# A fused four-layer kernel with the step order of all engines written out anew

## What is computed

```python
def first_block(x, ...):
    for layer in range(2):
        h = rmsnorm(x, norm_mix_g[layer])
        if layer % 2 == 0:
            mix = retention_nsa_mixer(h, ...)      # retention (4 heads) and NSA attention (8 heads)
        else:
            mix = hgrn2_mixer(h, ...)              # 8 heads of gated linear attention
        x = x + mix
        h = rmsnorm(x, norm_ffn_g[layer])
        x = x + (silu(h @ ffn_w1[layer]) * (h @ ffn_w3[layer])) @ ffn_w2[layer]
    return rmsnorm(x, final_norm_g)

def second_block(x, ...):
    for l in range(2):
        mix = diff_attention(x, ...) if l == 0 else chunk_attention(x, ...)   # the second with a bias table
        x = layer_norm(alpha * x + mix, ...)
        x = layer_norm(alpha * x + swiglu_2(x, ...), ...)
    return x

def reference(...):
    return second_block(first_block(x, ...), ...)
```

## Time and profile before

| | before |
|---|---|
| time, median of three runs | 1376.7 us (1375.18 to 1377.59) |
| the profiled execution | 1377.06 us |
| its span | 1375.3 us |
| PE matmuls busy | 1330.7 us, 97% |
| PE weight loads busy | 1095.0 us, 80% |
| POOL busy | 1033.3 us, 75% |
| ACT busy | 717.1 us, 52% |
| DVE busy | 383.5 us, 28% |
| mean granted clock of PE | 0.984 |
| DMA queue of the weights | 223.57 MB, 53.2% of 16 engines' span |
| chain that ended last | PE 88%, DVE 3%, POOL 3%, ACT 3%, DMA 2%, issue 2% |

### The profile page before, as it was taken

The page is one execution under the profiler, slowest core; times in us unless marked ns, Lnnn a source line. Parts: engine busy times, 40 slices in busy tenths (PEclk is TensorE's granted clock), DMA queues, the critical chain, the costliest instruction groups (busy, mean ns, idle before and its releaser), DMA issues.

```text
span 1375.3 us, 19563 instructions
## 1 busy us (share of the span) xinstructions
PE 1330.7 (97%) x7558; PEld 1095.0 (80%) x7558; DVE 383.5 (28%) x812; ACT 717.1 (52%) x1259; POOL 1033.3 (75%) x875
## 2 busy tenths in 40 slices
PE   6999999999999999999999998999999999999997
PEld 4888788888878777888887777788887788788886
DVE  1155421111157653110104463301103232411112
ACT  6355564454478776544444664444534554544431
POOL 6354878887885467888888776788879877788874
PEclk9799999999999999999999999999999999999999
DMA  8232456665644244666665643566656545466652
GB/s 272 92 108 77 138 172 184 188 196 172 193 158 124 79 123 128 201 190 183 180 191 158 184 125 122 154 214 186 196 173 209 182 140 153 139 214 187 197 170 89
DMA packets 63117, 224.92 MB, mean 164 GB/s; under 512 B 7345, under 2 KB 7985, under 8 KB 63025
## 3 DMA queue, kind: packets, MB, share of 16 engines
q1 hardware_dynamic: 62736, 223.57, 53.2%
q10 hardware_dynamic: 288, 0.10, 0.0%
HBM read 222.59 MB, written 1.05 MB: 163 GB/s over the span
## 4 chain that ended last, share of the span: by engine, by line
PE 88%; DVE 3%; POOL 3%; ACT 3%; DMA 2%; issue 2%; DVEq 0%; SPq 0%; ACTq 0%
PE G L1037 25%; PE G L1044 25%; PE G L1038 25%; POOL wlo L2180 3%; PE A L1211 2%; PE A L1068 1%; ACT whi L1913 1%; PE A L1146 1%; PE G L1211 1%; PE A L1182 1%; PE A L1058 1%; PE A L1080 1%; DMA raw<-in_w_e 0%; DMA raw<-in_w_a 0%; PE A L1320 0%
## 5 line engine op out<-in xcount | busy, mean ns | idle before, releaser
L2180 POOL TENSOR_TENSOR wlo<-raw,whi 128x256 fp32r<-128x256 f32 (+1 forms) x867 | 1023.7, 1218 | 324.0 <-ACT whi L1913 323.9
L1913 ACT ACTIVATE whi<-raw 128x1024 fp32r<-128x1024 f32 x403 | 425.1, 1060 | 357.3 <-PE G L1044 334.4
L1037 PE MATMUL G<-whi,xh 128*128 128x512 f32 (+2 forms) x1200 | 464.9, 391 | 9.2 <-DVE xl L1392 6.8
L1038 PE MATMUL G<-whi,xl 128*128 128x512 f32 (+2 forms) x1200 | 452.0, 380 | 0.0
L1044 PE MATMUL G<-wlo,xh 128*128 128x512 f32 (+2 forms) x1200 | 353.2, 380 | 1.3 <-POOL wlo L2180 1.3
L1037 PEld LDWEIGHTS G<-whi,xh 128*128 128x128 f32 x1200 | 228.3, 190 | 52.2 <-ACT whi L1913 7.6
L1038 PEld LDWEIGHTS G<-whi,xl 128*128 128x128 f32 x1200 | 228.6, 190 | 37.7
L1044 PEld LDWEIGHTS G<-wlo,xh 128*128 128x128 f32 x1200 | 219.9, 190 | 46.6 <-POOL wlo L2180 3.2
L1037 PE MATMUL G<-whi,hh 128*128 128x512 f32 x352 | 139.4, 396 | 0.0
L1038 PE MATMUL G<-whi,hl 128*128 128x512 f32 x352 | 138.8, 394 | 0.0
L1044 PE MATMUL G<-wlo,hh 128*128 128x512 f32 x352 | 110.4, 395 | 0.0
(11 more groups left out here) (340 smaller groups left out, 1196.7 us busy)
## 6 DMA issues: line engine op xcount, KB each, us to landing
raw<-in_g SPq DMA_DIRECT2D x88, 512.0 KB, 3.9
raw<-in_u SPq DMA_DIRECT2D x88, 512.0 KB, 4.0
raw<-in_d SPq DMA_DIRECT2D x88, 512.0 KB, 4.2
raw<-in_w_h SPq DMA_DIRECT2D x32, 512.0 KB, 3.6
raw<-in_w_e SPq DMA_DIRECT2D x24, 512.0 KB, 3.7
raw<-in_w_a SPq DMA_DIRECT2D x24, 512.0 KB, 3.6
raw<-in_w_b SPq DMA_DIRECT2D x24, 512.0 KB, 3.8
raw<-in_w_eo SPq DMA_DIRECT2D x8, 512.0 KB, 3.6
```

Source lines behind the costliest of these rows:

```text
L1037: e.matmul(o, sh[:, kt, xs], whi[h][:, ws], start=u.first and j == 0, stop=False)
L1038: e.matmul(o, sl[:, kt, xs], whi[h][:, ws], start=False, stop=False)
L1913: e.activation(whi[c % NH][:, 0:n], raw[c % NR][:, 0:n], ACT.Copy).then_inc(s_hi, 1)
L2180: m = e.tensor_tensor(wlo[c % NH][:, i:j], raw[c % NR][:, i:j], whi[c % NH][:, i:j].bitcast(F), ALU.subtract)
```

## The change

Only the text `PLAN` is changed, that is, the order in which each engine takes its steps. No operation, shape, buffer, semaphore or wait is changed, and each stage has the steps that it had. What differs:

- In all four mixers the lines are drawn up anew: a step stands behind another unit, or at another place among the steps of its unit. Side tiles change with it.
- On ACT a step that is to run ahead of a unit's split now stands one line earlier, since the splits come last in a line. So EV 0 1 stands in line 6 of stage 0, ahead of the splits of line 7, and SI in an odd line of the FFNs.
- The first six splits of stage 0 stand otherwise among the squares (SQ) and XH.
- At the borders of stages XH of the second half, or of both halves, stands behind the last split.

The diff of `PLAN`, cut to the lines that matter:

Stage 0, the start, the compression and the end of its first products:

```diff
--1: -XT 0 0; -SQ 0 0; -XT 1 0; -XH 0 0; -XH 1 0; -XL 0 0; HI 0; -XL 1 0; HI 1; HI 2
-0: -SQ 1 0; -SQ 0 1; -XT 0 1; HI 3; -XT 1 1
-1: -XH 0 1; -XH 1 1; -XL 0 1; -RS 0; -XL 1 1
-2: -SQ 1 1; HI 4; -RS 1
-3: HI 5
-4: EV 0 0; MB; QT 0 @0
-5: QC 0
-8: EV 0 1; QT 1 @1
-9: QC 1
+-1: -XT 0 0; -SQ 0 0; -XT 1 0; -XH 0 0; HI 0; -XL 0 0; -XH 1 0; HI 1; -XL 1 0
+0: HI 2; -XT 0 1; -SQ 0 1; -XT 1 1; HI 3
+1: -XH 0 1; -XH 1 1; -XL 0 1
+2: -SQ 1 0; -XL 1 1; -SQ 1 1; -RS 0
+3: HI 4
+4: HI 5; -RS 1
+5: EV 0 0
+6: EV 0 1; QC 0; QC 1
+7: MB; QT 0 @0
+8: QT 1 @1
-16: EV 1 1; TT 2 @2; TT 0 @0; TT 1 @1; TC 2
-17: TC 0; SC 1 0 0 @2; TC 1; CA 0 @0; MK 1 0 0; EX 1 0 0; CA 1 @1; CB 0; CE 0; TR 1 0 0; CD 0
-18: CPA 1 0 0; CB 1; CF 0; EV 2 0; AV 1 0 0; CG 0; CE 1
-19: CD 1; CF 1; SC 1 0 1 @0; CG 1; SC 0 0 0 @1; MK 1 0 1
...
+14: EV 1 1
+15: TC 2; TC 0; TC 1; EV 2 0; EX 1 0 0
+16: TT 2 @2; TT 0 @0; TT 1 @1
+17: SC 1 0 0 @2
+18: MK 1 0 0; CA 0 @0; CA 1 @1; CB 0; CE 0; CD 0; CF 0; CB 1; TR 1 0 0
+19: CPA 1 0 0; CG 0; CE 1; AV 1 0 0; CD 1; SC 1 0 1 @0; CF 1; MK 1 0 1
...
-54: EV 6 1
-55: GS 1; GT 1
-57: GU 1; R8 0; R8 1; MT 2 @1
+52: EV 6 1
+54: GS 1
+55: GT 1
+57: GU 1; R8 0; R8 1; MT 2 @0
```

Stage 1, the gate's silu of block 0, second half (likewise in every block of every FFN):

```diff
-8: SI 0 1
+7: SI 0 1
```

Stage 2:

```diff
-8: EV 0 1; FB 0 @1
-9: FA 0
-11: FD 0
-12: EV 1 0; FE 0
-14: FF 0
-16: EV 1 1; FG 0; FB 1 @2
-18: FA 1; FJ 0
-19: T1 0 @0; EV 2 0; FD 1; H1 0 0 @1; TV 0
-20: TA 0
-22: H1 0 1 @0
-23: H2 0 0
-24: H2 0 1; H3 0 0
-25: FE 1; H3 0 1; H4 0 0; EV 2 1; FF 1; H4 0 1; HA 0 0
-26: HA 0 1; H5 0 0
-27: FG 1; H5 0 1; GB 0 @1; H1 1 0 @0; GC 0; FJ 1
-29: GF 0; H2 1 0; H1 1 1 @2; T1 1 @1; H2 1 1; H3 1 0
-30: H3 1 1; H4 1 0; TA 1; H4 1 1; H5 1 0
-31: H5 1 1; HA 1 0; HA 1 1; TV 1; EV 3 0; H1 2 0 @0; EV 3 1; H1 2 1 @2; H2 2 0
-32: H2 2 1; H3 2 0; H1 3 0 @1
-33: H3 2 1; H2 3 0; H4 2 0; H3 3 0; H4 2 1; HA 2 0; H5 2 0; FB 2 @0; H4 3 0; HA 2 1; H5 2 1; FA 2
-34: H5 3 0; H1 3 1 @2
-35: HA 3 0; FD 2; H2 3 1; O1 0 @1; FE 2; H3 3 1; EV 4 0; FF 2; H4 3 1; O2 0
...
-38: FJ 2; MT 0 @2
-39: MH 0; T1 2 @1; ML 0; H1 4 0 @0; TV 2; TA 2; H1 4 1 @2
...
+7: B3; EV 0 1
+9: FB 0 @1
+10: FA 0
+12: EV 1 0; FD 0
+14: FE 0; EV 1 1
+16: FF 0
+18: FB 1 @2; FG 0
+19: FA 1; FJ 0
+21: T1 0 @0; FD 1; H1 0 0 @1; FE 1; TV 0
+22: TA 0; H2 0 0; FG 1; H2 0 1; EV 2 0; HA 0 0; EV 2 1
+23: FF 1; H1 0 1 @0; H3 0 0; H4 0 0; FJ 1
+24: H5 0 0; H3 0 1; H1 1 0 @2; H1 1 1 @1; H2 1 0; H4 0 1; H2 1 1; H3 1 0
+25: HA 0 1; H5 0 1; H4 1 0; H3 1 1; T1 1 @0; HA 1 0
+26: H5 1 0; TA 1; GB 0 @2; H4 1 1
+27: GC 0; H5 1 1; TV 1
+28: HA 1 1; EV 3 0; H1 2 0 @1
+29: H2 2 0; GF 0; H1 2 1 @0; H3 2 0; H1 3 0 @2
+30: H2 2 1; H2 3 0; H3 2 1; H4 2 0; H3 3 0
+31: HA 2 0; H5 2 0; H4 2 1; EV 3 1; FB 2 @1; H4 3 0; H5 2 1
+32: HA 2 1; HA 3 0; FA 2; H5 3 0; H1 3 1 @0; O1 0 @2; H2 3 1; FD 2; FE 2; H3 3 1
...
+36: EV 4 0; FJ 2; MT 0 @0
+37: MH 0; T1 2 @2; ML 0; H1 4 0 @1; TV 2; H1 4 1 @0
+38: TA 2; H2 4 0; H2 4 1; EV 4 1; H2 5 0
...
-56: EV 6 1; FG 3; GB 2 @2; O1 2 @0; GC 2; FJ 3
-57: O2 2; GF 2; T1 3 @1
-58: TV 3; TA 3; H1 6 0 @2
+58: O1 2 @0; GB 2 @2; GC 2; T1 3 @1; GF 2; O2 2
+59: TV 3; TA 3; H1 6 0 @2
...
```

The end of stage 3, then the beginning of stage 4:

```diff
-130: RS 0
-131: AP 0 0; RES 1 1; XT 0 0; AP 1 0; XH 0 0; XT 1 0; SQ 1 1; XL 0 0; XH 1 0
+129: RS 0
+130: AP 0 0
+131: AP 1 0; XT 0 0; RES 1 1; XT 1 0; XL 0 0; XL 1 0
...
-0: -RS 1; -XL 1 0; -AP 0 1
-1: -AP 1 1; -XT 0 1; MB; P1; -XT 1 1; -XH 0 1
-2: -XH 1 1; -XL 0 1; P2; -XL 1 1
-3: P3
-4: RO 0 0
+0: -XH 0 0; -XH 1 0; -SQ 1 1; -RS 1; -AP 0 1
+1: -AP 1 1; -XT 0 1
+2: -XH 0 1; MB; -XT 1 1
+3: -XL 0 1; -XH 1 1; P1
+4: -XL 1 1; P2
+5: RO 0 0
+7: P3
```

Stage 4, blocks 1 and 5 and the last heads:

```diff
-16: CPA 0 0; EV 1 1; AV 0 0; TR 0 1
+14: CB2 0 1; CPA 0 0
+15: AV 0 0; TR 0 1; EV 1 1; NQ 0 0; CPA 0 1
...
-45: EV 5 0; RC 3 0; CB2 3 0; AV 2 0
-46: NQ 2 0; TR 3 0
-47: NF 2 0; CPA 3 0
-48: EV 5 1; AV 2 1; AV 3 0
-49: NQ 2 1
-50: NQ 3 0; NF 2 1
-51: NF 3 0; MT 2 @1; DC 3 1 @0; MH 2
-52: MK 3 1
-53: ML 2; EX 3 1
-55: RC 3 1; CB2 3 1
-56: TR 3 1
-57: CPA 3 1; AV 3 1; NQ 3 1; NF 3 1; MT 3 @1; MH 3; ML 3
+44: EV 5 0
+45: RC 3 0; CB2 3 0; AV 2 0; TR 3 0
+46: NQ 2 0; CPA 3 0
+47: NF 2 0; AV 3 0; EV 5 1; NQ 3 0
+48: AV 2 1; NF 3 0
+49: NQ 2 1; DC 3 1 @1; NF 2 1
+50: MK 3 1; MT 2 @0; EX 3 1
+51: MH 2
+52: RC 3 1; CB2 3 1
+54: ML 2; TR 3 1
+55: CPA 3 1; AV 3 1
+56: NQ 3 1
+57: NF 3 1; MT 3 @0; MH 3; ML 3
```

The end of stage 5 and the beginning of 6, and two EV of stage 6:

```diff
-131: AP 1 0; XT 0 0; RES 1 1; XT 1 0; XH 0 0; BN 1 1; XH 1 0; XL 0 0; AG 1
+131: AP 1 0; XT 0 0; RES 1 1; XT 1 0; BN 1 1; XL 0 0; AG 1
...
-0: -XL 1 0; -RS 1; -AP 0 1
+0: -XH 0 0; -XH 1 0; -XL 1 0; -RS 1; -AP 0 1
...
-8: EV 0 1; KT 0 @0
+7: EV 0 1
+8: KT 0 @0
...
-24: EV 2 1; KT 1 @1
+23: EV 2 1
+24: KT 1 @1
```

## The result

The changed kernel took 1353.4 us (median of four runs, 1350.83 to 1355.25), the kernel before 1375.94 (four runs, 1375.07 to 1377.59). The ratio is 0.984 (95% interval 0.982 to 0.986): 22.5 us less, where 17 were forecast, and inside the stated range.

What follows compares the result with a forecast made beforehand. TensorE (PE) bounds everything, so order gives only its waits, half-clock stretches and switching. 7.8 + 1.4 + 0 + 1.0 + 2.1 + 5.4 + 0.3 = 18.0, less 1: 1377.06 - 17 = 1360 us, range 1352 to 1369.

Steps and rivals of the forecast that it cites:

- the 1 us held back: Whole kernel: 1 us taken off the 18.0 summed gain for waits not found in four rewritten mixers, leaving 17.
- Part 1: Stage 0: EV 0 1 ahead of splits ends the wait at QT 1, 7.8 us gained; other evictions and R8, 1.4.
- Part 2: Stage 0 compression burst (CA 0, CA 1): unit 18 ahead of it, up to 0.7 us, taken as 0; low stretch may move.
- rival (a): Stage 0: clock does not fall after CA, the waits before it being gone; 1353 us, chance 0.09.
- Part 3: Stage 2: T1 0 behind unit 21 removes its wait; new waits of 4.5 us follow; net 1.0 gained, between -5 and +4.
- Rival (d): Stage 2: Part 3's wait comes at all four TAs, each 4.5 + 2.9 us; slower, 1381 us, chance 0.04.
- Part 4: Stages 3 to 4: 2.1 us gained at the border, 5.4 in stage 4 from evictions, CPA 0 0, MT 3 and the clock.
- Part 5: The rest, odd stages, later borders and stage 6: +0.3 us, with 0.9 gained in stage 6 less 0.2 for a switch.
- Rival (b): Stage 4 and twice in stage 2: low clock stretches return, plus an unfound wait; 1366 us, chance 0.20.
- Rival (c): Stage 0: chunk landings set the pace if PE outruns the loads, 5 us go; 1365 us, chance 0.06.
- signs named: Stages 0, 2, 4: no QT 1 wait, unit 12 about 31, stage 2 waits 4 to 5, about 11 us in even stages.
- sign of being wrong: Clock of 1.0 from 50 to 65 us, stage 2 waits above 9, or stage 0 products waiting for a split or POOL.

Runs made afterwards that it cites:

- the compression in two pieces: Changed kernel with CA 0 behind unit 17 and CA 1 behind unit 19 of stage 0, two units between the halves of the burst: 1359.0 us, ratio 0.988.
- MT 2 late: Changed kernel with MT 2 of stage 0 behind unit 59 instead of 57 and MT 3 behind unit 60: 1353.5 us, ratio 0.984.
- the changed kernel again: The changed kernel, nothing altered, run once more on the chip of three variants of it: 1353.9 us, ratio 0.984.
- the three together: Changed kernel with R1/MT tiles exchanged and MT 2, MT 3 later, TA 0 and followers ahead of the split, EV 0 1 ahead of split 7: 1347.2 us.

## Why the forecast was right, and where it was off

The total stands on its largest term, 7.8 us, which was right. In the table above the kernel beats the forecast by 6.4 us in some stretches (1.6, 0.8, 0.9, 1.6, 0.1 and 1.4) and falls short of it by 2.6 in others (0.8, 0.4, 0.2 and 1.2). That is 3.8 more than forecast, and the 1 us held back comes on top. Not all of these are the order's work, as the parts below say: how much of the 1.6 at the start is its work stays open, and the 1.2 lost in stage 7 do not come from it.

**Part 1 (EV before the splits)** held: 7.0 for 7.8. The difference is a wait of 0.6 at QT 1 that I had at none:

```profile
24.02 1.06 ACT L1926 ACTIVATE whi<-raw 128x1024 fp32r<-128x1024 f32 x1 [2.59 <-DMA raw<-in_w_e]
24.98 0.67 ACT L1939 ACTIVATE PJ<-G,SM 128x512 f32<-128x512 f32 x1
25.55 0.59 ACT L2007 ACTIVATE QT<-A 128x512 f32<-128x512 f32 x1
```

I took over the landing of chunk 7 from the earlier trace rows and let EV 0 1 follow it; the chunk landed 0.4 earlier, PE was 1.6 earlier. The start I had not looked at: HI 0 goes ahead of XH 1 0, and the first product of 8.83 begins at 7.62. How much of that is the order stays open, since in the other variants with the new start it began between 7.61 and 8.96. The rest of stage 0 gave 2.2, where the evictions and R8 were to give 1.4; 0.4 of that came back in stage 1, where some of the XT now stand.

**Part 2 (compression)**: 0 was right, and so was "the low stretch may move with it". From unit 12 to unit 50 the profiled execution took 108.4 us, against 109.0 before, and the wait of 0.7 at TT covers that. It was luck as well: the second profile of the same kernel took 106.9 there, with a shorter low stretch. The clock fell 3 us into the burst (at 43.7) with PE busy throughout, so rival (a) failed.

The Trainium skill's account of such falls by waits between groups of matmuls (TensorE: Matmul & The Clock Gate, HAM oscillation), as I applied it here, failed in this trace too. What the burst has in all traces is matmuls of 1 to 30 columns. The window of the low stretch:

```profile
43.70:57.40 13.70, 13.70 (x104) 13.42 (x103) 4.33 (x19) 2.07 (x5) 3.35 (x5) 0.50 0.13 40
```

**Part 3 (stage 2)** had the mechanism and its sizes: 1.9 for 1.0. Of the difference, 0.6 is that the three waits were 3.9 and not 4.5. Rival (d) did not come: no later TA made PE wait. That the low clock cost as much as before was so in this execution (6.8 us in both); with the same text of stage 2 it was low for 3.4 us in the trace with the compression in two pieces.

**Part 4**: the border gave 1.9 for 2.1, with 1.6 of waits left and not 0.6. The step that was mis-sized is "Its chain ... then ends before unit 57 does ... costing about 2.4": from unit 44 to unit 62 the kernel gained 5.9, of which 2.8 are idle time (0.4, 0.3, 2.1), and the other 3.1, not 2.4, fall to the low stretch of 6.8 us, which went with the wait. The other 0.9 of the 1.6 by which this part was off lie between units 6 and 44: the kernel gained 1.1 there, where the 0.6 of CPA 0 0 less 0.4 for "two switches more" made 0.2. And "0.6" for CPA 0 0 was one execution's value of a wait that reaches 2.9.

**Part 5**: "0.9, for one switch more, 0.2" in stage 6 was the wrong term: 2.1, in two traces. A wait of 0.37 before KT was worth 0.56 in the length of its unit (2.71 to 2.15), and the rest is how the small matmuls stand among the units; I had priced a switch by one number, 0.2, which no row gave, and the count of switches does not carry it. As a mean it was not far off: KT 0 with eight matmuls makes its unit longer by 0.79 (2.15 less 1.36), QT 1 with four by 0.47 (1.83 less 1.36, with MT 2 late) and the unit behind it by 0.11, which leaves some 0.26 for the switch, an estimate.

**Rival (b)** came in part: the clock fell at the border to stage 7, for 3.4 us and 1.2 us of time. The kernel with the new stage 6 alone does not have it, two kernels with the old stage 6 do, and in two variants the clock fell at the border to stage 6 instead. So it belongs to the execution and not to the order. **Rival (c)** came as the 0.6 us at QT 1 and no more.

Of the signs named, unit 12 (30.3 for "about 31"), T1 0, MT 3 and the 1.5 behind it came as said. QT 1 waited 0.6, where none was to be seen, and the three waits of stage 2 are 3.9, just under the "4 to 5". One sign of being wrong, a product that waits for a split or POOL in stage 0, is there, but only at the start, where it was before, and smaller. The 11 us of waits in the four windows are 14.5, of which 5.8 (2.9 and 2.9) lie at the borders to stages 5 and 7, which the windows did not reach before. The 1 us held back for waits not found was the wrong way round.

## What to carry to other kernels

On an engine that runs in order and whose work partly waits for transfers, a step that the bottleneck waits for belongs ahead of each step that waits for a landing, even if the trace shows that landing in time: the next execution may not. But look at what is put behind it: TA 0 ahead of FE 1 began the chain to FJ 1 later, and PE waited 8.5 us. A wait removed shows the next one behind it, so look up every holder of the same tile or buffer before you move a step. What a wait is worth is read from the length of the units around it, and includes the clock after it, which may go one way in one execution and the other in the next.

## What the runs showed of the hardware

The same steps had low stretches of quite different lengths behind the compression burst. The window from 40 to 62 us of four traces, with MT 2 late, of the changed kernel again, of the changed kernel, and with the three together:

```profile
40.00:62.00 22.00, 22.00 (x213) 20.26 (x212) 8.31 (x32) 10.61 (x38) 5.89 (x9) 0.84 0.28 91
```

```profile
40.00:62.00 22.00, 22.00 (x205) 20.50 (x204) 7.18 (x28) 9.10 (x34) 5.83 (x9) 0.77 0.30 96
```

```profile
40.00:62.00 22.00, 22.00 (x196) 20.73 (x195) 6.51 (x24) 7.75 (x26) 6.09 (x9) 0.69 0.29 93
```

```profile
40.00:62.00 22.00, 22.00 (x186) 20.34 (x184) 5.90 (x21) 6.91 (x23) 5.55 (x8) 0.61 0.28 88
```

Means of 0.84, 0.77, 0.69 and 0.61 are 7.0, 10.1, 13.6 and 17.2 us at 1.2 GHz, and from unit 16 to unit 32 these executions took 56.44, 58.02, 59.52 and 61.09 us. So each microsecond at the lower clock costs 0.46 here ((61.09 - 56.44) / (17.2 - 7.0)), and this one place spreads the time by 4.65 us, though the steps between these units are the same. Four more traces have these steps: they took 56.4, 59.5, 59.6 and 61.1 us, each close to one of these four. The changed kernel's ten executions spread by 6. An effect of less than about 2 us therefore needs many of them.

What sets the length is not shown.
